# GpSimd sums half of the modulation chunks of attention's head loop, and one matmul with split operands spreads each head's decays

## The reference

```
cond = silu(c)
for layer in 0, 1:
    mod = cond @ ada_w[layer] + ada_b[layer]         # 6 shifts, scales and gates of width 1024
    h = modulate(rms_norm(x), sh_m, sc_m)
    mix = sparse attention(h) if layer == 0 else gated DeltaNet(h)
    x = x + g_m * mix
    h = modulate(rms_norm(x), sh_f, sc_f)
    x = x + g_f * peer_ffn(h)                        # product keys, top 16, gathered experts
return rms_norm(x, final_norm)
```

```
g = -exp(a_log) * softplus(a_raw + dt_bias)          # (512 tokens, 16 heads)
g = cumsum(g) within a chunk
decay = exp(g[..., :, None] - g[..., None, :])       # lower triangle only
```

## Time and profile before

| what | value |
|---|---|
| median of 3 runs | 3538.48 us (3535.4 to 3541.85) |
| span of the profiled execution | 3545.4 us, 62942 instructions |
| PE busy | 3445.5 us (97%) |
| DVE busy | 2618.3 us (74%) |
| ACT busy | 1782.3 us (50%) |
| POOL busy | 1146.3 us (32%) |
| attention's head loop | from about 176 to 289 us of the span |
| the delta rule's head loop | from about 1642 to 1892 us of the span |

### The profile page before, as it was taken

The page is one execution under the profiler, slowest core; times in us unless marked ns, Lnnn a source line. Parts: engine busy times, 40 slices in busy tenths (PEclk is TensorE's granted clock), DMA queues, the critical chain, the costliest instruction groups (busy, mean ns, idle before and its releaser), DMA issues.

```text
span 3545.4 us, 62942 instructions
## 1 busy us (share of the span) xinstructions
PE 3445.5 (97%) x20002; PEld 3168.1 (89%) x20002; DVE 2618.3 (74%) x4805; ACT 1782.3 (50%) x3234; POOL 1146.3 (32%) x866
## 2 busy tenths in 40 slices
PE   7998999999999999998999999999999999999998
PEld 5656899999999999997776787799999999999998
DVE  5864768579987888886888443567569996888886
ACT  3474355567773333336884233445557775333333
POOL 0302342534441222223663002443434442222222
PEclk9999999999999999999999999999999999999999
DMA  8463355889999999992557642345699999999995
GB/s 301 139 207 120 100 164 172 283 307 361 371 381 371 347 346 343 352 346 74 171 174 204 163 134 78 88 127 172 213 342 317 374 378 367 358 339 339 339 341 209
DMA packets 519872, 914.10 MB, mean 258 GB/s; under 512 B 70352, under 2 KB 359248, under 8 KB 511312
## 3 DMA queue, kind: packets, MB, share of 16 engines
q1 hardware_dynamic: 446032, 644.23, 53.1%
q0 software_dynamic: 73728, 268.47, 21.2%
HBM read 782.54 MB, written 130.02 MB: 257 GB/s over the span
## 4 chain that ended last, share of the span: by engine, by line
PE 84%; ACT 5%; DVE 4%; DMA 3%; issue 2%; SPq 1%; POOL 0%; DVEq 0%; ACTq 0%
PE bank L835 10%; PE bank L833 10%; PE bank L834 10%; PE bank L905 10%; PE bank L906 10%; PE bank L907 10%; PE bank L881 5%; PE bank L1060 2%; PE bank L498 2%; PE bank L1069 1%; DMA w_ring<-b_w_in 1%; DVE oh L2738 1%; PE bank L617 1%; PE bank L844 1%; PE bank L1134 1%
## 5 line engine op out<-in xcount | busy, mean ns | idle before, releaser
L833 PE MATMUL bank<-hx,hl 128*128 128x384 f32 (+1 forms) x2304 | 797.9, 346 | 0.8 <-POOL hl L1649 0.8
L835 PE MATMUL bank<-hx,hl 128*128 128x384 f32 (+1 forms) x2304 | 786.0, 341 | 0.0
L834 PE MATMUL bank<-hx,hl 128*128 128x384 f32 (+1 forms) x2304 | 785.5, 341 | 0.0
L905 PE MATMUL bank<-W,hl 128*128 128x384 f32 x2016 | 681.2, 338 | 6.3 <-DVE W L2776 6.3
L907 PE MATMUL bank<-W,hl 128*128 128x384 f32 x2016 | 680.8, 338 | 0.0
L906 PE MATMUL bank<-W,hl 128*128 128x384 f32 x2016 | 680.7, 338 | 0.0
L1672 POOL DMA_INDIRECT rows<-p_v,erow x256 | 262.0, 1024 | 860.7 <-DVE xtok L2783 838.7
L1672 POOL DMA_INDIRECT rows<-p_u,erow x256 | 358.1, 1399 | 405.9 <-DVE rows L2709 368.0
L1996 ACT ACTIVATE hl<-hT 128x1024 fp32r<-128x1024 f32 x272 | 287.7, 1058 | 364.8 <-PE bank L907 318.8
L1996 ACT ACTIVATE hl<-w_ring 128x1024 fp32r<-128x1024 f32 x272 | 287.5, 1058 | 347.5 <-PE bank L907 313.5
L833 PEld LDWEIGHTS bank<-hx,hl 128*128 128x128 f32 x2304 | 434.2, 188 | 11.1 <-POOL hl L1649 1.0
(11 more groups left out here) (386 smaller groups left out, 5540.1 us busy)
## 6 DMA issues: line engine op xcount, KB each, us to landing
w_ring<-p_u_t SPq DMA_DIRECT2D x128, 512.0 KB, 5.4
hT<-p_u_t SPq DMA_DIRECT2D x128, 512.0 KB, 6.1
w_ring<-p_v SPq DMA_DIRECT2D x128, 512.0 KB, 6.3
hT<-p_v SPq DMA_DIRECT2D x128, 512.0 KB, 6.8
act_scratch<-hT SPq DMA_DIRECT2D x256, 192.0 KB, 4.3
g_scratch<-gst SPq DMA_DIRECT2D x48, 1024.0 KB, 6.9
gg<-g_scratch SPq DMA_DIRECT2D x64, 768.0 KB, 7.3
ua<-act_scratch SPq DMA_DIRECT2D x256, 192.0 KB, 5.6
```

The lines of the kernel that those rows point to most:

```text
L833: nc.tensor.matmul(bank[s][:, c:], hi, hx[:, 0, k, c:], start=(k == 0), stop=False)
L834: nc.tensor.matmul(bank[s][:, c:], hi, hx[:, 1, k, c:], start=False, stop=False)
L835: mm = nc.tensor.matmul(bank[s][:, c:], lo, hx[:, 0, k, c:], start=False, stop=(k == KD - 1))
L905: nc.tensor.matmul(bank[j][:, P:], hi, W[:, s, 0, :], start=first, stop=False)
```

## The change

Attention: the eight even half chunks stay with TensorE, in the steps of `ROWS_AT` = 4, 7, 10, ... 25. The eight odd ones are summed by GpSimd (`half_sums`): a multiplication of the chunk with `cond` in place (128x2048 elements), then three additions (1024, 512 and 256 elements a partition), the last into `rstd`. TensorE only adds over the partitions (`half_columns` with an odd `n`), in the steps of `SUMMED_AT` = 8, 11, 15, 18, 22, 25, 29, 32. All odd chunks pass through slot 1 of `half_ring`, and the next is loaded when GpSimd's four instructions on the one before are done.

Delta rule: `sums_` holds the cumulative decays of all 16 heads by row, the high parts in rows 0 to 15 and the low parts in rows 32 to 47; `pick` holds the column that selects a head's two rows. `decays` is then one matmul of 512 columns. `select` and `gsel` go away. The table is made ahead of the loop.

```diff
-HALF_AT = [VALUE_STEPS + m for m in range(3 * HALVES // 2) if m % 3 < 2]
+ROWS_AT = [VALUE_STEPS + 3 * m for m in range(HALVES // 2)]
+SUMMED_AT = [2 * VALUE_STEPS + 7 * m // 2 for m in range(HALVES // 2)]
...
                 def half_columns(n):
-                    pe.wait_ge(psum_free[7], base[7] + VALUE_STEPS + n + 1)
+                    if n % 2:
+                        pe.wait_ge(sem("half_summed"), 4 * (n // 2) + 4)
+                    else:
+                        pe.wait_ge(psum_free[7], base[7] + VALUE_STEPS + n // 2 + 1)
...
-                    if m - 1 in HALF_AT:
-                        mm = half_columns(HALF_AT.index(m - 1))
-                        if m - 1 == HALF_AT[-1]:
-                            mm.then_inc(sem("halves_turned"), 1)
-                    if m in HALF_AT:
-                        half_rows(HALF_AT.index(m))
+                    if m - 1 in ROWS_AT:
+                        half_columns(2 * ROWS_AT.index(m - 1))
+                    if m in SUMMED_AT:
+                        half_columns(2 * SUMMED_AT.index(m) + 1)
+                    if m in ROWS_AT:
+                        half_rows(2 * ROWS_AT.index(m))
...
+                take(3)
+                for tt in range(TT):
+                    for r in (0, NARROW):
+                        mm = nc.tensor.matmul(bank[3][r:r + VH, tt * P:(tt + 1) * P], graw[:, tt, :], tri[:, :],
+                                              start=True, stop=True)
+                mm.then_inc(psum_full[3], 1)
...
                 def decays(i, a):
-                    pe.wait_ge(sem("gsel_ready"), i + 1)
+                    if i == 0 and a == 0:
+                        pe.wait_ge(sem("sums_split"), 2)
                     take(2 + a)
-                    for tt in range(TT):
-                        mm = nc.tensor.matmul(bank[2 + a][:, tt * P:(tt + 1) * P],
-                                              gsel[:, tt, a:a + 1].to_broadcast([P, P]), tri[:, :],
-                                              start=True, stop=True)
-                    mm.then_inc(psum_full[2 + a], 1)
+                    n = 2 * i + a
+                    nc.tensor.matmul(bank[2 + a][:, :], pick[:, n:n + 1].to_broadcast([P, P]), sums_[:, :],
+                                     start=True, stop=True).then_inc(psum_full[2 + a], 1)
...
             def load_half(n):
-                if n >= 2:
-                    sp.wait_ge(psum_full[7], marks["heads"][7] + VALUE_STEPS + n - 1)
+                if n >= 2 and n % 2:
+                    sp.wait_ge(sem("half_summed"), 4 * (n // 2))
+                elif n >= 2:
+                    sp.wait_ge(psum_full[7], marks["heads"][7] + VALUE_STEPS + n // 2)
...
+            def half_sums(n):
+
+                pool.wait_ge(sem("half_loaded1"), 16 * (n // 2 + 2))
+                part = half_ring[:, 1, :, :]
+                nc.gpsimd.tensor_tensor(part, part, cond[:, :, 0:1].to_broadcast([P, KD, HALF]), ALU.mult
+                                        ).then_inc(sem("half_summed"), 1)
+                for step, width in enumerate((4, 2, 1)):
+                    pool.wait_ge(sem("half_summed"), 4 * (n // 2) + step + 1)
+                    if width == 1 and n > 3:
+                        pool.wait_ge(sem("halves_turned"), n // 2 - 1)
+                    to = part[:, 0:width, :] if width > 1 else half_sum(n).unsqueeze(1)
+                    nc.gpsimd.tensor_tensor(to, part[:, 0:width, :], part[:, width:2 * width, :], ALU.add
+                                            ).then_inc(sem("half_summed"), 1)
+
+            for n in range(1, HALVES, 2):
+                half_sums(n)
             for s in range(2):
                 pool.wait_ge(sem(f"high_done{s}"), marks["attn_out"][f"split{s}"] + 1)
...
-                    if m in HALF_AT:
+                    if m in ROWS_AT:
                         evac(7, half_part[:, :], bank[7][:, 0:HALF])
-                    if m in (HALF_AT[-1] + 2, HALF_AT[-1] + 4):
-                        out_high((m - HALF_AT[-1]) // 2 - 1)
+                    if m == ROWS_AT[-1] + 3:
+                        out_high(0)
+                    if m == PAIR_STEPS + LAG - 1:
+                        act.wait_ge(sem("half_summed"), 4 * (HALVES // 2))
+                        out_high(1)
...
+                nc.scalar.activation(pick[:, :], stacked[:, :], ACT.Copy).then_inc(sem("sums_split"), 1)
+                full(3)
+                act.wait_ge(sem("gdn_masks"), 3)
+                for r in (NARROW, 0):
+                    nc.scalar.activation(sums_[r:r + VH, :], bank[3][r:r + VH, :], ACT.Copy).then_inc(sem("sums_high"), 1)
                 act.wait_ge(sem("gdn_from_dve"), 3)
...
+                dve.wait_ge(sem("sums_high"), 2)
+                c = slice(NARROW, NARROW + VH)
+                nc.vector.tensor_tensor(sums_[c, :], bank[3][c, :], sums_[c, :].bitcast(F32), ALU.subtract
+                                        ).then_inc(sem("sums_split"), 1)
+                dve.wait_ge(sem("sums_split"), 2)
+                dve.sem_inc(psum_free[3], 1)
                 dve.wait_ge(sem("gdn_from_act"), 3)
```

More of the change, by code:

```diff
@@ L341, in hybrid_trunk @@
         cy = sb("cy", [P, 2, 4, T], where=solve_)
-        gsel = sb("gsel", [P, TT, 2], where=solve_)
+        pick = sb("pick", [P, NARROW], F32R, where=solve_)
+        sums_ = sb("sums", [P, T], F32R, where=solve_)
         BS = sb("BS", [P, 2, TT, P], where=solve_)
@@ L439, in hybrid_trunk, with half_sum @@
         late_bank = (3, 4, 5, 2)
+        def half_sum(n):
+            q = n // 2 % 2 * HALF
+            return rstd[:, q:q + HALF]
         def out_raw(m):
@@ L722, in half_rows @@
                 def half_rows(n):
-                    pe.wait_ge(sem(f"half_loaded{n % 2}"), 16 * (n // 2 + 2))
+                    pe.wait_ge(sem("half_loaded0"), 16 * (n // 2 + 2))
                     take(7)
@@ L726, in half_rows @@
                         r = 32 * (k % 4)
-                        mm = nc.tensor.matmul(bank[7][r:r + 32, 0:HALF], cond[:, k, :], half_ring[:, n % 2, k, :],
+                        mm = nc.tensor.matmul(bank[7][r:r + 32, 0:HALF], cond[:, k, :], half_ring[:, 0, k, :],
                                               start=(k < 4), stop=(k >= KD - 4))
@@ L731, in half_columns @@
                 def half_columns(n):
-                    pe.wait_ge(psum_free[7], base[7] + VALUE_STEPS + n + 1)
+                    if n % 2:
+                        pe.wait_ge(sem("half_summed"), 4 * (n // 2) + 4)
+                    else:
+                        pe.wait_ge(psum_free[7], base[7] + VALUE_STEPS + n // 2 + 1)
+                    part = half_sum(n) if n % 2 else half_part
                     for c in range(2):
                         col = HALF + 2 * D // P + 2 * n + c
-                        mm = nc.tensor.matmul(bank[7][:, col:col + 1], half_part[:, c * P:(c + 1) * P], ones[:, 0:1],
+                        mm = nc.tensor.matmul(bank[7][:, col:col + 1], part[:, c * P:(c + 1) * P], ones[:, 0:1],
                                               start=True, stop=True)
-                    return mm
+                    if n % 2:
+                        mm.then_inc(sem("halves_turned"), 1)
                 def outputs(hp):
@@ L935, in deltanet @@
                 mark("gdn_heads")
-                for b in (2, 7, 7):
+                for b in (2, 3, 7, 7):
                     marks["gdn_heads"][b] += 1
@@ L1695, in deltanet @@
                 pool.wait_ge(sem("x_ready"), 2)
+                nc.gpsimd.memset(sums_[:, :].bitcast(F32), 0.0)
                 nc.gpsimd.memset(tri[:, :], 1.0)
@@ L1707, in deltanet @@
                 pool.wait_ge(sem("gdn_from_dve"), 4)
-                t.n.update(marks["gdn_heads"])
-                base = marks["gdn_heads"]
                 wide = [P, TT, P]
@@ L1713, in column @@
                     return of[:, :, n:n + 1].to_broadcast(wide)
-                def select(i):
-                    if i > 0:
-                        pool.wait_ge(psum_full[2], base[2] + i)
-                        pool.wait_ge(psum_full[3], base[3] + i)
-                    nc.gpsimd.tensor_copy(gsel[:, :, :], graw[:, :, 2 * i:2 * i + 2]).then_inc(sem("gsel_ready"), 1)
                 def betas(i):
@@ L1742, in deltanet @@
                     if i < KH:
-                        select(i)
                         head_low(4 * i + 3)
@@ L2540, in attention @@
                 output_low(KD - 1)
-                dve.wait_ge(sem("halves_turned"), 1)
+                dve.wait_ge(sem("halves_turned"), HALVES // 2)
                 nc.vector.tensor_copy(mods[:, 1, 0:G_M], adab[:, 1, 0:G_M])
```

## The result

The changed kernel takes 3572.57 us (median; 3564.17 to 3589.18) against 3538.43 us for the kernel before in the same session (3532.45 to 3546.39). The ratio is 1.0098, 95% interval 1.0074 to 1.0122: about 1% slower. The forecast was 3567, range 3553 to 3583. The number held; the mechanism that it was built on was only one of two, and not the one that set the pace.

A forecast was written before the change was run, and what follows sets the result against it. TensorE was taken to set the head loop's pace; after the change, GpSimd's chain of load and sum would. 25.0 + 1.7 + 3.4 - 1.3 = +28.8 us on 3538.5 gives 3567.3, say 3567; range 3553 to 3583.

The forecast's parts named there:

- out_tile(0) at +25.0: Output projection's start: waits for GpSimd's last sum and first low part, at 303.9 where it was 278.90, +25.0 us.
- clock at +1.7: Head loop: TensorE's granted clock falls in its waits, costing once, behind the last wait, +1.7 us.
- The chain of load and sum: Head loop, slot 1: GpSimd's sum (8.8 us) and the load (5.3) alternate, 14.5 us a turn, and set the pace.
- It is near, but GpSimd's chain is slower: Head loop: VectorE, blocked beside GpSimd, gets 4.1 steps through a turn where 3.5 are wanted, so it doesn't pace.
- rival B: Head loop: VectorE's instructions blocked by GpSimd set the pace, turns of 16.5 to 17 us, 3577 to 3590; chance 0.14.
- 4.1 steps a turn: Head loop: VectorE's steps a turn, 1.3 during GpSimd's sum and 2.8 during the load, where 3.5 are wanted.
- lower bound of 13.8: Head loop: shortest turn of load and sum, with the load landing in 5.1 us and nothing pushed in by VectorE.
- rival A: Head loop: the forecast itself, GpSimd's chain of load and sum sets the pace, 3553 to 3577; chance 0.76.
- Start: Delta rule ahead of its loop: eight more small matmuls, two ScalarE copies and the table load delay the first tap, +3.4 us.
- The -1.3 us of the last turn: Delta rule's loop: only the two shortened `decays` of the last turn, on the chain, give time back, -1.3 us.
- Rival C: Head loop and delta rule: sums keep up, TensorE's 8 us and the delta rule's 7 are gained, 3523; chance 0.03.
- Rival D: Late sum made up behind the loop, or delta rule gives all back with GpSimd somewhat quicker: 3539 to 3553; chance 0.07.

The follow-up runs named there:

- third: Kernel before, with GpSimd doing the sum's four instructions eight times on a spare buffer nobody reads: head loop 131.34 us, ratio 1.0063.
- fifth runs: Kernel before, with the same idle GpSimd work, and VectorE's `nmx` and divisions also writing an unused sum: head loop 103.42 us, ratio 1.0010.
- fourth run: Attention's part alone, with VectorE's `nmx` and divisions also writing an unused sum: head loop 124.07 us, ratio 1.0058 against the kernel before.
- ninth run: Attention's part with a second odd-chunk slot, `nmx` and divisions also writing a sum, loads 12 and 15 exchanged: 3532.53 us, ratio 0.9979 against the kernel before.

## Why the prediction was right, and where it was not

**The sign and the size, right.** +25.7 us in the head loop, where out_tile(0) at +25.0 and clock at +1.7 were forecast. The agreement has luck in it: two limits of nearly the same size stood beside each other, and the forecast priced one of them, and that one too high. By its measured parts the chain alone would have put out_tile(0) at 297.8 on the scale of the kernel before (below), +18.9 us; the held-up VectorE made up the difference. The medians differ by 34.1 us, 5.3 more than forecast. The loop's 25.7 and the delta rule's 2.6 are 28.3 of them; the rest is assigned to no stage, and the spans of the two traces differ by 27.9.

**The chain of load and sum: a real limit, but not the one that bound.** The step that failed is the sentence "It is near, but GpSimd's chain is slower". VectorE's blocked instructions set the pace, which was rival B, given 0.14. The last sum was ready 7.6 us before it was used. TensorE was to wait for `rstd` about seven times, 25 to 35 us in all; no such wait is in the trace, and its idle time was 21.4 us. Rival B's price, 3577 to 3590, was too high in turn: it took turns of 16.5 to 17 us, and GpSimd's stayed at 13.6.

**Why 4.1 steps a turn was too many.** The count took VectorE as a queue that only has to get its work done: 1.3 steps in a sum, 2.8 in a load. By its busy time, 105.2 us of 128.9, it was indeed not full. What the count left out is that one step's work goes VectorE (`nmx`), ScalarE (exponentials), VectorE (division), TensorE (transposes), with each of the two VectorE parts held up by a whole GpSimd instruction at a time, and the order keeps only three steps in flight. ScalarE's 6.81 us of idle time behind one `nmx` is such a case. That this is why a not quite full VectorE paces the loop is argued from these rows; that the blocking is the cause is shown by the third and fifth runs.

The Trainium skill, in SBUF — State Buffer, section Who interferes with whom, counts `tensor_scalar` among the instructions that can take the shared ports, but not the form that also writes out its accumulator. The traces agree on both: a mean of 588 ns for `nmx` in the changed kernel with the one form, and 154 in the fourth run with the other.

**The parts of a turn.** The multiplication took 3.62 us, forecast 4.2: mis-sized, since it was placed between a full addition and a small multiplication with two broadcasts. The sum is 8.2 (8.8), the load 5.3 as forecast, the turn 13.6 (14.5), below the lower bound of 13.8. (By its own terms, 8.8 + 5.1 + 0.1, that bound is 14.0; and rival A's terms add up to about 3551 to 3575, not 3553 to 3577. Neither slip decides anything.) The low part was ready at 295.4, which is 297.8 on the scale of the kernel before, whose loop began 2.4 us later; it was forecast for 303.9.

**TensorE's clock, wrong in kind.** Forecast: +1.7 once, behind the last wait. Measured: 0.84 over the whole loop, 17 us of slower matmuls. It was low in or right behind stretches in which TensorE was idle for 2 to 3 us in 10 (0.66 in 220 to 230, 0.59 in 240 to 250), though 1.00 in 230 to 240 with 3.0 us idle, and it was 1.00 over the loop of the ninth run, with 5.5 us idle in 96. How much of the 25.7 us the slow matmuls add and how much they only fill of the waits wasn't taken apart and stays open.

**The delta rule, right in the main.** Start +2.6 for +3.4: the eight small matmuls (16 records) took 1.05 us and not 1.78, the copies 1.20 for 1.1, and the unhidden table load 1.28 as forecast. The turns didn't move, as forecast. The -1.3 us of the last turn came and went again: from its L1016 to the first product with the next weights (`gs`) it was 13.7 us for 14.9, but to the last of these products 66.1 for 65.8. The freed time went partly to a wait that wasn't named, VectorE's low part of the weights, and not to more waiting for `cy` (9.3 us for 9.6).

**Rival C.** Its condition, a turn of at most 8.8 us, can't be had with one slot. With two slots and the other form GpSimd's sums follow each other every 8.2 us where TensorE lets them, and nearly all of the 8 us are there. The loop then is 7.2 us shorter than before, in the ninth run.

**Rival D.** The late sum was not made up behind the loop: from the first output matmul to the first peer stage it was 68.2 us, 69.0 before.

## What to carry to other kernels

Before work is given to an idle GpSimd, list what VectorE runs beside it: instructions that took 0.2 to 0.5 us alone took up to 3.7 here, and the loss can exceed the work that was moved (25.7 us against 8 here). Changing the form of VectorE's instructions cost 0.2 us here and saved 28. When a cure moves the time little, look for a second limit of the same size before the first theory is dropped; two cures crossed with each other in four kernels tell it plainly.

## What the runs showed of the hardware that was not expected

- A multiplication of 2048 elements with one operand broadcast took 3.62 us on GpSimd, an addition of 2048 with two full operands 4.60.
- VectorE held up GpSimd hardly at all: the pair of additions took 3.69 to 3.81 us in all eight sums, while divisions went from 415 to 831 ns.
- ScalarE's two copies of 16 rows of 512 from PSUM took 1.20 us, 0.60 each, the same as one of 128 rows; VectorE's two took 1.40.
- The granted clock went from 1.00 to 0.59 between neighbouring stretches of 10 us, 230 to 240 and 240 to 250, in which TensorE was busy 6.99 and 8.68 us; with a mean of 0.59, both levels, 1.2 and 2.4 GHz, lie within the second one.
